# Gate and up of ten feed-forward blocks by seven Strassen products of halves, down a block later, g through transposes

## What is computed

```python
...
        x = x + g1 * (y @ w_out[layer])
        h2 = rms_norm(x, norm2_gain[layer]) * (1 + sc2) + sh2
        ffn = (jax.nn.silu(h2 @ ffn_w_gate[layer]) * (h2 @ ffn_w_up[layer])) @ ffn_w_down[layer]
        x = x + g2 * ffn
```

## Time and profile before

| | us |
|---|---|
| median of 3 runs | 2435.54 (2428.57 to 2438.64) |
| the profiled execution | 2432.71 |
| its span, first to last instruction | 2431.0 |

### The profile page before, as it was taken

One profiled execution on the slowest core, in us unless ns is written; L12 is line 12 of the kernel. 1 busy time (PEld: TensorE's weight loads), 2 busy tenths in 40 slices (PEclk: granted clock), 3 DMA queues, 4 the chain that ended last, 5 costly groups with the idle time before them and its releaser, 6 DMA issues.

```text
span 2431.0 us, 27509 instructions
## 1 busy us (share of the span) xinstructions
PE 2382.3 (98%) x10811; PEld 1948.5 (80%) x10811; DVE 1151.7 (47%) x1548; ACT 685.3 (28%) x987; POOL 82.4 (3%) x80
## 2 busy tenths in 40 slices
PE   6999999999999999999999999999999999999998
PEld 5877787888876788788888888888888888888887
DVE  5977876577666433533333333333333433333334
ACT  4243325233146322422222212121222222222212
POOL 0011101111001000000000000000000000000000
PEclk8999999999999999999999999999999999999999
DMA  9976780877620332233323333232333233333233
GB/s 343 314 244 220 271 302 13 285 255 235 203 71 18 144 99 96 80 98 100 95 95 95 97 101 95 95 95 95 98 101 95 95 95 95 99 99 95 95 95 104
DMA packets 177996, 329.39 MB, mean 135 GB/s; under 512 B 14457, under 2 KB 59999, under 8 KB 176776
## 3 DMA queue, kind: packets, MB, share of 16 engines
q1 hardware_dynamic: 177928, 328.47, 41.2%
HBM read 320.02 MB, written 11.03 MB: 136 GB/s over the span
## 4 chain that ended last, share of the span: by engine, by line
PE 94%; DVE 3%; DMA 1%; SPq 1%; ACT 1%; issue 1%; ACTq 0%; DVEq 0%
PE PS L587 26%; PE PS L589 26%; PE PS L588 26%; PE PS L751 2%; PE PS L727 2%; PE PS L594 2%; PE PS L596 2%; PE PS L595 2%; DMA ada_first<-in_ada_w 1%; DVE acc_first L1368 1%; PE PS L742 1%; DVE wlo L1317 1%; PE PS L872 1%; PE PS L616 0%; SPq L398 0%
## 5 line engine op out<-in xcount | busy, mean ns | idle before, releaser
L587 PE MATMUL PS<-hhi,whi 128*128 128x512 f32 x2176 | 859.4, 395 | 11.3 <-DVE hlo L1709 3.9
L589 PE MATMUL PS<-hhi,wlo 128*128 128x512 f32 x2176 | 851.5, 391 | 0.0
L588 PE MATMUL PS<-hlo,whi 128*128 128x512 f32 x2176 | 851.4, 391 | 0.0
L1395 DVE TENSOR_TENSOR wlo<-stage,whi 128x1024 fp32r<-128x1024 f32 x240 | 294.2, 1226 | 860.5 <-ACT whi L1048 860.5
L1048 ACT ACTIVATE whi<-stage 128x1024 fp32r<-128x1024 f32 x240 | 254.6, 1061 | 1007.3 <-PE PS L589 1007.3
L587 PEld LDWEIGHTS PS<-hhi,whi 128*128 128x128 f32 x2176 | 411.7, 189 | 99.9 <-issue 9.8
L589 PEld LDWEIGHTS PS<-hhi,wlo 128*128 128x128 f32 x2176 | 411.2, 189 | 86.6
L588 PEld LDWEIGHTS PS<-hlo,whi 128*128 128x128 f32 x2176 | 411.9, 189 | 84.1 <-issue 0.7
L1317 DVE TENSOR_TENSOR wlo<-stage,whi 128x1024 fp32r<-128x1024 f32 x144 | 183.0, 1272 | 272.9 <-ACT whi L1042 272.6
L1042 ACT ACTIVATE whi<-stage 128x1024 fp32r<-128x1024 f32 x144 | 152.5, 1061 | 496.9 <-PE PS L589 398.9
L587 PE MATMUL PS<-ghi,whi 128*128 128x512 f32 x704 | 274.0, 389 | 1.5 <-DVE xT L1733 1.5
(11 more groups left out here) (244 smaller groups left out, 1432.1 us busy)
## 6 DMA issues: line engine op xcount, KB each, us to landing
ada_ring<-in_ada_w SPq DMA_DIRECT2D x128, 512.0 KB, 4.9
stage<-in_ffn_w_gate SPq DMA_DIRECT2D x88, 512.0 KB, 3.5
stage<-in_ffn_w_up SPq DMA_DIRECT2D x88, 512.0 KB, 3.4
stage<-in_ffn_w_down SPq DMA_DIRECT2D x88, 512.0 KB, 3.6
stage<-in_w_in SPq DMA_DIRECT2D x80, 512.0 KB, 6.1
ada_first<-in_ada_w SPq DMA_DIRECT2D x64, 512.0 KB, 6.9
stage<-in_w_out SPq DMA_DIRECT2D x32, 512.0 KB, 3.7
xnat<-in_x SPq DMA_DIRECT2D x4, 1024.0 KB, 7.9
```

Of the source, the lines that this page charges most:

```text
L587: mm(PS[:, b, :], whi[:, slot, kk, cols], rhi, start=start, stop=False)
L588: mm(PS[:, b, :], whi[:, slot, kk, cols], rlo, start=False, stop=False)
L589: return mm(PS[:, b, :], wlo[:, slot, kk, cols], rhi, start=False, stop=stop)
L1395: v.tensor_tensor(wlo[:, j % NW, :, :], stage[:, j % NSTAGE, :, :], whi[:, j % NW, :, :].bitcast(F32), ALU.subtract).then_inc(w_lo, 1)
```

## The change

Gate and up of blocks 1 to 10 are computed by Strassen's scheme on a 2 x 2 split: tokens in two halves of 256, model columns in two halves of 1024 (`A11`, `A12`, `A21`, `A22`), and, as the two columns of the weight matrix, gate and up (B11 and B21 are the two halves of gate, B12 and B22 those of up). Seven products of halves replace eight. Four sums of activations (`S1` to `S4`) are made once; four sums of weights are made for each block on VectorE, in the stage slots, before the chunk is rounded (`t1`, `t2`, `t3`, `minus_t4`, each one or two operations on 128 x 1024).

- A block has 36 positions (NPOS), each one chunk of 512 KB: 28 are chunks of products with 12 matmuls each, 8 are chunks of down with 24. Positions 0 to 7, 10, 13, 16 and 19 are the first three products (`SET1`), 8, 9, 11, 12, 14, 15, 17 and 18 are down of the block before (`DOWN_AT`), and 20 to 35 are the other four products (`SET2`), in four groups of four. Down of a block therefore comes one block later.
- Stage has six slots (NRING). A slot whose chunk is still wanted by a later sum is freed later (`SUM_AFTER`). `whi` and `wlo` keep two buffers.
- In a product the activations are stationary and the weights move (`split_tile`), so the result has tokens on the partitions. VectorE combines the seven products from pairs of PSUM banks (`u_first`, `u_plus_m5`, `c22`, `c11`, `c21`, `u_plus_m7`, `c12`, 2 operations each), ScalarE takes silu in SBUF, VectorE multiplies (`g_upper`, `g_lower`). TensorE transposes g, 16 transposes of 128 x 128 a block in two halves (`g_transposes`), and ScalarE and VectorE split it from PSUM (`f_high`, `f_low`).
- Down has its weight chunk as 512 rows by 256 columns, two output tiles at a time in banks 6 and 7 (`down`, `down_out`).
- Block 0 is computed with all eight products, gate and up interleaved chunk by chunk, while the activations are written: seven quarter tensors kept of each tile pair in `xc_hi` and `xc_lo`, A21 in a ring of four.
- The last down sends the tokens back in five parts instead of four, and `ostage` holds all four column groups.

The diff's core:

```diff
+C_FF0 = GCH * G_FF
+C_FF1 = C_FF0 + 2 * GCH
+NPOS = 36
+NRING = 6
+HT = S // 2
+S1, S2, S3, S4, A11, A12, A22, A21 = range(8)
+DOWN_AT = (8, 9, 11, 12, 14, 15, 17, 18)
+SET1 = ((0, 1, 2), (3, 4, 5), (6, 7, 10), (13, 16, 19))
+SET2 = ((20, 21, 22, 23), (24, 25, 26, 27), (28, 29, 30, 31), (32, 33, 34, 35))
+SUM_AFTER = {1: 1, 3: 1, 4: 1, 6: 1, 7: 2, 13: 1, 16: 1}
+PB, QB, RB, WB = 0, 2, 4, 6
...
+            def free_slot(n, p):
+
+                later = SUM_AFTER.get(p - NRING, 0)
+                sp.wait_ge(w_lo, chunk_of(n, p) - NRING + 1 + later)
...
+            def product(n, p, q, j, bank0, free):
+
+                pe.wait_ge(w_lo, chunk_of(n, p) + 1)
+                for t in range(2):
+                    if j == 0:
+                        pe.wait_ge(bank_free[bank0 + t], free)
+                    for kk in range(CK):
+                        cols = slice(P * t, P * (t + 1))
+                        last = split_tile(bank0 + t, xc_hi[:, CK * j + kk, q, cols], xc_lo[:, CK * j + kk, q, cols],
+                                          whi[:, p % NW, kk, :], wlo[:, p % NW, kk, :],
+                                          j == 0 and kk == 0, j == 3 and kk == 1)
+                last.then_inc(w_used, 1)
...
+            pe.wait_ge(xs_lo, GCH)
+            with pe.Fori(0, NFB - 1) as n:
+                for p in range(SET2[0][0]):
+                    if p in DOWN_AT:
+                        down(n, p, DOWN_AT.index(p))
+                        continue
+                    j = [p in js for js in SET1].index(True)
+                    if p == SET1[j][0]:
+                        product(n, p, A11, j, PB, p_base + 2 * n)
+                    elif p == SET1[j][1]:
+                        product(n, p, S1, j, RB, r_base + 2 * n)
+                    else:
+                        product(n, p, S2, j, QB, p_base + 2 * n)
+                    if p == SET1[1][2]:
+                        for b in range(2):
+                            pe.wait_ge(bank_free[WB + b], w_free(n))
+                        g_transposes(n, 0, WB)
+                    if p == SET1[2][0]:
+                        pe.wait_ge(g_lo, 4 * n + 2)
+                        g_transposes(n, 1, WB)
+                for j in range(4):
+                    t3, b21, t4, b22 = SET2[j]
+                    product(n, t3, S3, j, WB, w_free(n) + 8)
+                    product(n, b21, A12, j, PB, p_base + 1 + 2 * n)
+                    product(n, t4, A22, j, QB, p_base + 1 + 2 * n)
+                    product(n, b22, S4, j, RB, r_base + 1 + 2 * n)
...
+            def hi_at(n, p, down=False):
+
+                if p in SUMMED and not down:
+                    act.wait_ge(w_sum, sums_of(n, p))
+                else:
+                    act.wait_ge(stage_in[p % NRING], landed_at(n, p))
+                act.wait_ge(w_used, chunk_of(n, p) - NW + 1)
+                f(whi[:, p % NW, :, :].rearrange("p k n -> p (k n)"), slot_of(p), ACT.Copy).then_inc(w_hi, 1)
...
+            def t1(n, j):
+                b11, p, _ = SET1[j]
+                in_stage(n, b11, p)
+                v.tensor_tensor(slot_of(p), slot_of(p), slot_of(b11), ALU.subtract).then_inc(w_sum, 1)
...
+            def t3(n, j):
+                p, _, b11, b22 = SET2[j]
+                in_stage(n, p, b22)
+                v.tensor_tensor(slot_of(p), slot_of(b22), slot_of(p), ALU.subtract).then_inc(w_sum, 1)
+                in_stage(n, b11)
+                dve.wait_ge(w_sum, sums_of(n, p))
+                v.tensor_tensor(slot_of(b11), slot_of(b11), slot_of(p), ALU.add).then_inc(w_sum, 1)
```

More of the change, by code:

```diff
@@ L497, in _ @@
+            up_w = A["ffn_w_up"][0].rearrange("(h k p) n -> p h k n", p=P, h=2)
             down_w = A["ffn_w_down"][0].rearrange("(k p) n -> p k n", p=P)
[L499 to L522, removed]
+            for kp in range(GCH):
+                for m, w in enumerate((gate_w, up_w)):
+                    c = C_FF0 + 2 * kp + m
+                    free_stage(c)
+                    sp.dma_start(stage[:, c % NSTAGE, :, :], w[:, :, kp, 0:CW]).then_inc(stage_in[c % NSTAGE], 16)
@@ L933, in _, with split_tile @@
             pe.wait_ge(rh_done, 1)
[L936 to L947, removed]
+            def split_tile(b, x_hi, x_lo, w, w_l, start, stop):
+                mm(PS[:, b, :], x_hi, w, start=start, stop=False)
+                mm(PS[:, b, :], x_hi, w_l, start=False, stop=False)
+                return mm(PS[:, b, :], x_lo, w, start=False, stop=stop)
@@ L1001, in _ @@
+            for e in range(GCH):
+                down(n, e, e, (lambda: by_token(3)) if e == GCH - 1 else None)
+                if e in (2, 4, 6):
+                    by_token(e // 2 - 1)
+            by_token(4)
         @block.scalar
@@ new lines, in _ @@
+            for t in range(4):
+                dve.wait_ge(bank_free[4 + t], r_base)
+            dve.sem_inc(g_ready, 4)
+            lo_at(0, 3)
+            t1(0, 1)
+            lo_at(0, 4)
+            t2(0, 1)
+            lo_at(0, 5)
+            with dve.Fori(0, NFB - 2) as n:
+                from_six(n)
+                lo_at(n + 1, 0)
+                c21(n)
+                c12(n)
+                lo_at(n + 1, 1)
+                t2(n + 1, 0)
+                lo_at(n + 1, 2)
+                lo_at(n + 1, 3)
+                t1(n + 1, 1)
+                lo_at(n + 1, 4)
+                t2(n + 1, 1)
+                u_plus_m7(n)
+                lo_at(n + 1, 5)
+                g_upper(n)
+                g_lower(n)
@@ L1766, in _ @@
+            n = NFB - 2
+            from_six(n, False)
+            lo_at(n + 1, 0)
+            c21(n)
+            u_plus_m7(n)
+            c12(n)
+            g_upper(n)
+            g_lower(n)
+            lo_at(n + 1, 1)
+            n = NFB - 1
+            f_low(n, range(2), 0)
+            f_low(n, range(2, 4), 2)
+            for e in range(GCH):
+                if e + 1 < GCH and e >= 1:
+                    lo_at(n, e + 1)
+                down_out(n, e, e)
             for t in (1, 3):
-                dve.wait_ge(fin_pe, 12 + t + 1)
```

594 lines of the change are left out of this document (424 added, 170 removed).

## The result

| | before | after |
|---|---|---|
| median of the runs, us | 2435.36 (2428.57 to 2438.64) | 2466.68 (2463.43 to 2472.66) |
| profiled execution, us | 2432.71 | 2472.66 |
| its span, us | 2431.0 | 2471.0 |

The ratio is 1.0134, with a 95% interval of 1.0118 to 1.015: slower by 1.3%, where 1.4 to 1.5% was forecast (2469). The profiled execution is the slowest of the four and reaches the feed-forward 4.3 us later than the one of before (974.15 against 969.88 for the stage's first matmul on `ssf`). Over the traces of all the kernels shown here this start varies between 966.8 and 975.9, and it is late in slow and fast kernels alike; what follows is therefore taken from waits and periods inside the stage.

What follows compares the result with a forecast made beforehand. PE, 98% busy, was taken as the bound, with the chain feeding it binding on shorter chunks. -89.6 + 72.8 + 40.8 + 3.0 + 9.2 = +36 on 2432.7 gives 2469 us; forecast band 2456 to 2478, range 2424 to 2500.

Steps and rivals of the forecast that it cites:

- TensorE's work, -89.6: Gate and up of blocks 1 to 10: 480 matmuls fewer, -108.8 us, added transposes of g +19.2, net -89.6 us.
- The waits in a block: PE stalls on the feeding chain: 7.28 us a block in ten blocks, 4.53 at nine block changes.
- 24, 28, 32 behind t3: First chunks of second-set groups: two chained t3 sums precede the remainder, PE 0.91 us late each, 2.73 in all.
- 1, behind c21 and c12: Chunk 1 of the next block: four evacuations stand before its remainder, PE 0.87 us late.
- 2, behind t2: Chunk 2: its rounding waits for t2, which stands behind the late remainder of chunk 1, 0.78 us.
- 5, behind t2 and u_plus_m7: Chunk 5: its rounding follows t2, and u_plus_m7 comes on top, 0.80 us.
- low parts of g: Transposes of the second half: PE waits for f_low behind VectorE's queue, 1.9 us at a block change.
- hole ahead of 18: Second of two transfers lands late, delaying t3 and the evacuation PE needs: 3.7 us a block, low end 1.9.
- Price (4): After waiting for VectorE, PE is back at its pace 0.23 us after the operation's end.
- The clock: Rival: clock falls in chunk 18's hole, 1.8 us a block, +18, 2487; chance 0.22 including VectorE slower still.
- Start and tail, 9.2 and nothing: Block 0's vector work covered, nil to 0.5 us; bare g, low clock and transposes at the end make tail 9.2.
- The rival on the other side: Chunk chain does not bind; only chunk 18's 0.5, f_low and the tail stay: 2377 us, chance 0.15.

Runs made afterwards that it cites:

- e6: Changed kernel with the residual evacuation of 17 ahead of t3, three rounded-weight buffers and g's first two tiles ahead of position 7: 2376.96 us, 0.9766 of before.
- e7: e6 with the weight sums t2 of groups 0 and 1 earlier in VectorE's queue: 2372.29 us, 0.9754 of before.
- e1: Changed kernel with the residual evacuation of down position 17 ahead of the two weight sums t3 of group 0: 2425.76 us, 0.9979 of before.
- e8: Changed kernel with t2 of group 3 ahead of the remainder of 16, so transfers for 22 and 23 are no longer issued together: 2437.81 us.
- e4: Changed kernel with three buffers for the rounded weights instead of two, nothing moved: 2430.98 us, 0.9997 of before.
- e5: Changed kernel with rounding and remainders of g's first two tiles ahead of position 7's: 2453.68 us, 1.0092 of before.

## Why the prediction was right, step by step

**TensorE's work, -89.6.** Right, and shown by e6 and e7: where the waits are nearly gone, a block takes 123.6 us. 528 matmuls and the transposes are 121.4 by the prediction's prices, 9.2 less than the 130.6 of before. The 2.2 us above it are the one wait (0.76), the wider distances (1.2) and a rest of 0.2.

**The waits in a block, 11.8 predicted.** One block of after, from one hole to the next, took 1414.64 - 1281.26 = 133.4 and the following 133.2 (predicted: near 133). Less the 121.4 of work, 11.9 and 11.7 are waits. The parts:

| wait, a block | predicted, us | measured, us |
|---|---|---|
| 24, 28, 32 behind t3, each | 0.91 | 0.74 to 0.79 |
| 1, behind c21 and c12 | 0.87 | 0.76 to 0.78 |
| 2, behind t2 | 0.78 | 0.74 |
| 5, behind t2 and u_plus_m7 | 0.80 | 0.81 |
| low parts of g | 1.9 | 1.8 |
| hole ahead of 18 | 3.7 | 2.5 to 2.9, mostly 2.6 |
| restart and low clock after it | 0 (rival: 1.8) | 1.5 to 1.7, nine times of ten |
| the small ones (0.09 to 0.13 each) | 0.9 | about 1.1, as wider distances |

The measured values are what the matmuls came late, restart included. PE's waits list 0.5 where 0.77 were lost, for two reasons. The profile counts idle time from the end of the matmul before, 0.39 us after its start, though the next was due after 0.23; and the first matmul after a wait is followed only after 0.33 us. Price (4) had the sum of both right in kind and 0.06 too high: here TensorE starts 0.06 us after VectorE's end (0.13 at position 1) and is back at its pace after 0.17, not 0.23. The restart makes about a fifth of each of the 59 waits; the rest is the chain.

**The hole: the mechanism right, the size wrong.** The step that failed is the landing of the second transfer, taken as "784.87 - 782.74 = 2.1 after the first". It landed 1.3 after: the two were issued at 1273.12 and 1273.60, landing 3.6 and 4.4 later by the table of transfers (windows of one issue each), so at 1276.7 and 1278.0:

```profile
stage<-in_ffn_w_gate SPq DMA_DIRECT2D x1, 512.0 KB, 3.6
...
stage<-in_ffn_w_up SPq DMA_DIRECT2D x1, 512.0 KB, 4.4
```

Over the ten blocks of after the two landed 1.3 to 1.4 us apart. Counted from the end of chunk 16, the landing is at 4.8, between the low end (3.9) and the value taken (5.6). The pair of the earlier trace rows had 1.13 us between its issues, and its second 512 KB took 2.1 us more, 250 GB/s; here the window from 1276 to 1278 moved 362. One lone pair was a thin basis. By the fit of the Trainium skill that the prediction weighed (DMA: Bandwidth & Descriptors, "Anatomy of one DMA") the pair is in after 4.4 us, as an estimate, and chunk 18 costs 2.5. Measured were 4.9 after the first issue and 2.6, so it came nearer than the row, though the page gives that fit for transfers issued by GpSimd and these were issued by SyncE.

The chained sum was mis-sized too: it starts 0.03 after its predecessor's end (1278.06 + 1.23 to 1279.32), not 0.10.

**The clock: a rival that came true in part.** The prediction took idle of 3.4 us, placed between 3.04 (spared) and 3.86 (low), and left it out of the sum. The idle was only 2.3 to 2.8 and the clock still fell nine times out of ten. So the hole's 1.1 too much and the clock's 1.5 too little cancelled, which was luck. More of it lies in the baseline: the forecast was +36 on 2432.7, and against the 2435.4 of the result the change measured +31. A forecast 2 us from the median is better than its parts. e1 and e8 show that the low clock hangs on the hole.

**Pipelining on VectorE.** The Trainium skill's rule that the next operation does not start until the pipe is empty (VectorE: DVE Perf Modes, "The DRAIN you can't avoid") is not what the trace shows after the change either: 1279.32 to 1280.46 is 1.14 us for an operation of 1.22. The same section adds that a next operation that is not held starts earlier, which the prediction left out and which is what these rows show. It was right to take 1.15 from the rows.

**Start and tail, 9.2 and nothing.** From the end of the last product (about 2401.8) to the last instruction are 69.2 us; from the same point of before (2372.5) 58.5. The difference of 10.7 holds 1.75 of transposes, so 9.0 is left. The tail's idle of 5.8 and 2.1 was predicted as 6.1 and 2.1. Block 0 with seven quarter tensors cost no wait beyond the first (3.4 against the 3.9 of the earlier trace rows).

**The rival on the other side** (the chain does not bind, 2377) has the number of e6, 2376.96, by chance: e6 gets there by a buffer and two moves. As a forecast for the change it was wrong: `hi` does not start before the chunk two back is used.

## What to carry to other kernels

When an edit shortens the work that one staged chunk feeds, walk the feeding chain (release, round, remainder, start) and compare its length with the new chunk; each queue item ahead of the chunk's own comes on top, and an engine busy two thirds of the time can still be the bound. Put an evacuation that frees a bank ahead of anything that waits for a transfer, and give the first stage of the chain one buffer more than looks needed: here that, with g's first tiles moved ahead, made 1.3% slower into 2.3 to 2.5% faster. Moving a queue item ahead gains nothing where the wait only changes its place, as in e7, so read the period of the loop, not the place of the wait.

## What the runs showed of the hardware

- The granted clock fell to half after idle of 2.0 to 2.8 us on a TensorE that had been busy throughout, though the kernel before kept 1.00 through 3.04 us in its attention stage. Between 2 and 3 us the length did not decide, while the short holes were all spared: 9 of 10 holes in after, 10 of 10 in e4 (2.01 to 2.44 us), 5 of 10 in e5 (the longest, 2.81, spared), 0 of 10 at 0.91 to 1.29 in e8. Each fall cost 1.5 to 1.8 us. In after the first distance behind the hole was already long (0.5 to 0.6 us), in e4 TensorE had first gone back to 0.23. What decides between the two outcomes at the same length is open; it was not tried apart.
- A TensorE that had waited at full clock for VectorE started 0.06 us after the releasing operation's end (0.13 at position 1), and its second matmul came 0.33 us later, not 0.23. The lateness is about 0.27 us more than the idle that the profile lists.
- Matmuls without a wait are 0.2267 us apart before and 0.2290 on average in a block of e6. The cause is open.
- Two transfers of 512 KB issued 0.48 us apart landed 1.3 to 1.4 us apart, ten times, where two issued 1.13 us apart had landed 2.1 apart, once. Alone, the same transfer took 3.5 to 3.8 us (e8).
